# A hybrid attention block on eight cores: all GEMMs feature-major, gates per partition, norms by one ones-matmul, contiguous compression reads

## What is computed

```python
mod = jax.nn.silu(c) @ w_ada[l] + b_ada[l]                       # (B, 6D)
shift1, scale1, gate1, shift2, scale2, gate2 = [m[:, None, :] for m in jnp.split(mod, 6, axis=-1)]
h = _rmsnorm(x, norm1_g[l]) * (1.0 + scale1) + shift1
proj = h @ w_in[l]                                               # (B, T, D_IN)
nsa_q, nsa_kv, nsa_gate, fox_qkv, fox_f, merge_g = jnp.split(proj, SPLIT_POINTS, axis=-1)
...
o_nsa = _nsa(q_n, kv_n, nsa_gate, ...)      # compressed, selected and window attention, 16 heads, 4 kv groups
o_fox = _fox(q_f, k_f, qkv_f[:, :, 2], fox_f + b_forget[l])      # softmax attention with forget gates, 16 heads
g_merge = jax.nn.sigmoid(merge_g)
y = g_merge[..., :D] * (o_nsa @ w_up_nsa[l]) + g_merge[..., D:] * (o_fox @ w_up_fox[l])
x = x + gate1 * (y @ w_out[l])
h2 = _rmsnorm(x, norm2_g[l]) * (1.0 + scale2) + shift2
x = x + gate2 * (jnp.square(jax.nn.relu(h2 @ w_ff1[l])) @ w_ff2[l])
```

## Time and profile before

| what | value |
|---|---|
| median of 3 runs | 9671.58 us (9669.93 to 10086.41) |
| the profiled execution | 9690.02 us, its span 9688.5 us |
| busy in the span: TensorE, VectorE, ScalarE | 8696.5, 1708.3, 1575.5 us |
| span of the eight cores | 9649.9 to 9688.5 us |
| HBM read, written | 1604.60 MB, 138.41 MB |

### The profile page before, as it was taken

One profiled execution on the slowest core, in us unless ns is written; L12 is line 12 of the kernel. 1 busy time (PEld: TensorE's weight loads), 2 busy tenths in 40 slices (PEclk: granted clock), 3 DMA queues, 4 the chain that ended last, 5 costly groups with the idle time before them and its releaser, 6 DMA issues.

```text
span 9688.5 us, 111427 instructions; the slowest of 8 cores (9649.9 to 9688.5 us)
## 1 busy us (share of the span) xinstructions
PE 8696.5 (90%) x43283; PEld 3928.5 (41%) x43283; DVE 1708.3 (18%) x3599; ACT 1575.5 (16%) x2833; POOL 355.0 (4%) x676
## 2 busy tenths in 40 slices
PE   2287998999998887888889988999999999999999
PEld 1133333344444553333334443444444444444444
DVE  2012302210000112222222222311111111121112
ACT  2022202221002663222220011200000000000000
POOL 0000000000000000000000000000000000000000
PEclk6598998999999999999999999999999999999999
DMA  9955565785224664222224555445644764565455
GB/s 201 169 126 118 114 119 111 132 149 108 53 53 93 129 130 90 54 44 51 55 42 106 113 122 132 93 78 134 153 90 80 156 140 78 107 156 111 79 135 133
DMA packets 338516, 1049.97 MB, mean 108 GB/s; under 512 B 80928, under 2 KB 138688, under 8 KB 251728
## 3 DMA queue, kind: packets, MB, share of 16 engines
q0 software_dynamic: 96768, 700.33, 41.0%
q1 hardware_dynamic: 241232, 342.53, 11.4%
HBM read 1604.60 MB, written 138.41 MB: 180 GB/s over the span
## 4 chain that ended last, share of the span: by engine, by line
PE 79%; DMA 10%; DVE 5%; issue 3%; ACT 2%; SPq 1%; DVEq 0%; ACTq 0%; POOLq 0%
PE ps L335 78%; DMA ws_46<-w_ada 4%; DMA cx_48_90<-xc 2%; DMA rope_104<-rope 1%; DMA cx_47_89<-xc 1%; DMA ws_45<-w_inV 1%; PE ps L339 1%; SPq L371 0%; DVE onsa_141 L355 0%; DVE oaccS_140 L349 0%; DVE of_79_121 L349 0%; DVE oaccS_140 L355 0%; DMA xt_25_67<-xc 0%; DMA out<-x_131_173 0%; ACT pT_75_117 L342 0%
## 5 line engine op out<-in xcount | busy, mean ns | idle before, releaser
L335 PE MATMUL ps<-hown_61,ws_43 128*128 128x512 bf16 x2624 | 683.2, 393 | 5.5 <-DVE hown_61 L351 2.7
L335 PE MATMUL ps<-hown_61,ws_45 128*128 128x512 bf16 x2496 | 655.7, 396 | 0.0
L335 PE MATMUL ps<-hown_61,ws_44 128*128 128x512 bf16 (+1 forms) x2112 | 556.5, 399 | 0.0
L342 ACT ACTIVATE rl_157_199<-ps 128x512 f32<-128x512 f32 x128 | 76.4, 597 | 2129.2 <-PE ps L335 2129.2
L335 PEld LDWEIGHTS ps<-hown_61,ws_43 128*128 128x128 bf16 x2624 | 243.7, 100 | 256.7 <-issue 62.8
L335 PEld LDWEIGHTS ps<-hown_61,ws_45 128*128 128x128 bf16 x2496 | 233.6, 101 | 232.9 <-issue 51.1
L335 PE MATMUL ps<-ws_43,uT_189 128*128 128x512 bf16 x1408 | 321.8, 379 | 0.0
L335 PE MATMUL ps<-ws_155,uT_189 128*128 128x512 bf16 x1408 | 321.8, 379 | 0.0
L335 PE MATMUL ps<-x1T_165,ws_44 128*128 128x512 bf16 x1408 | 314.6, 382 | 4.2 <-ACT x1T_165 L342 2.6
L335 PE MATMUL ps<-x1T_165,ws_45 128*128 128x512 bf16 x1408 | 309.3, 381 | 0.0
L335 PE MATMUL ps<-wsx_201,uT_189 128*128 128x512 bf16 x1344 | 307.2, 379 | 0.0
(11 more groups left out here) (473 smaller groups left out, 10497.6 us busy)
## 6 DMA issues: line engine op xcount, KB each, us to landing
ws_44<-w_ada POOLq DMA_DIRECT2D x61, 1024.0 KB, 10.0
ws_45<-w_ada POOLq DMA_DIRECT2D x47, 1024.0 KB, 10.4
ws_44<-w_ff POOLq DMA_DIRECT2D x43, 1024.0 KB, 8.5
ws_45<-w_ff POOLq DMA_DIRECT2D x43, 1024.0 KB, 8.6
ws_43<-w_ff POOLq DMA_DIRECT2D x43, 1024.0 KB, 8.4
ws_155<-w_ff POOLq DMA_DIRECT2D x43, 1024.0 KB, 8.6
ws_43<-w_ada POOLq DMA_DIRECT2D x42, 1024.0 KB, 10.7
ws_46<-w_ada POOLq DMA_DIRECT2D x42, 1024.0 KB, 11.0
```

The lines of the kernel that those rows point to most:

```text
L335: S.emit(PE, lambda e: e.matmul(out_, lhsT, rhs, start=start, stop=stop, skip_group_check=True), reads, writes)
L342: S.emit(ACT, lambda e: e.activation(out=out_, in_=in_, func=func, **kw), reads, writes)
```

## The change

All GEMMs become feature-major. The host gives x transposed, as 32 tiles of 128 features, and takes `out` so; W_V, W_out and W_ff2 are tiled as the others.

- One `gemm` takes the place of both forms. It holds one slot; the last three column tiles of W_out and the first four of W_ff1 run as a group, half 0 of all, then half 1.
- A gate is now a column of `modT`, a scalar per partition: `stt` does product and sum in one, in W_out and W_ff2. The spread rows, `d_gate` and its loads go.
- Norms sum over partitions: squares are added up in a tile `acc` of 128 x 512 by ScalarE and VectorE (`add_square`), and one fp32 ones-matmul per 512 tokens gives the sum in all partitions (`rstd`). `modulate` is one VectorE product and one ScalarE scale and shift per 512.
- `ctx_build` loads each context tile once, 64 of 128 x 512, issued two steps ahead into three buffers. No transposes.
- `cmpx` is laid out so that a compression's operand is a run of 127.
- The rotation table: resident for q (`ropeO`); for keys three buffers loaded two ahead.
- V: `epi_v` copies on ScalarE, transposes 4 times, copies on VectorE, stores. `hold` is gone.

```diff
-    def ctx_build():
...
+        for j in range(-2, len(steps)):
+            if j + 2 < len(steps):
+                kc, t0, n = steps[j + 2]
+                x = tiles[j + 2] = cxr.next()
+                dma(SP, x.t[:, 0:n], xT_d[kc, :, t0:t0 + n], [], [x.b])
+            if j >= 0:
+                kc, t0, n = steps[j]
+                x = tiles.pop(j)
+                add_square(cacc, t0, n, x.t[:, 0:n], csq.next(), kc == 0, [x.b])
+                cp(DVE, hctx.t[:, kc, t0:t0 + n], x.t[:, 0:n], [x.b], rbs(hctx, kc, t0, n))
+            yield 1800
+        for t0, n in CC:
+            rstd(cacc, t0, n, PS[7])
+            yield 3000
+        for kc, t0, n in steps:
+            modulate(hctx, kc, t0, n, cacc, csq.next(), s1T, 0)
+            yield 1800
...
+    def gemm(srcs, ncol, places, ring, epilogue):
         ws = [slots.get(s) for s in srcs]
+        for tb, t0, n, idx in places:
+            for j, w in enumerate(ws):
+                p = ring.next()
+                for kc in range(32):
+                    mm(p.t[0:ncol, 0:n], w.t[:, ncol * kc:ncol * kc + ncol], tb.t[:, kc, t0:t0 + n], kc == 0, kc == 31,
+                       [w.b] + rbs(tb, kc, t0, n), [p.b])
+                    if kc % 2:
+                        tick(n / 1.2)
+                spawn(epilogue(p, j, idx))
+        for w in ws:
+            slots.put(w)
...
+    def add_square(acc, t0, n, x, sq, first, xb):
+        if first:
+            act(acc.t[:, t0:t0 + n], x, AF.Square, xb, [acc.b])
         else:
+            act(sq.t[:, 0:n], x, AF.Square, xb, [sq.b])
+            tt(DVE, acc.t[:, t0:t0 + n], acc.t[:, t0:t0 + n], sq.t[:, 0:n], ALU.add, [sq.b], [acc.b])
+    def rstd(acc, t0, n, bank):
+        a = acc.t[:, t0:t0 + n]
+        mm(bank.t[:, 0:n], onesf, a, True, True, [acc.b, cf.b], [bank.b])
+        act(a, bank.t[:, 0:n], AF.Ln, [epsc.b], [acc.b, bank.b], scale=1.0 / D, bias=epsc.t[:, 0:1])
+        act(a, a, AF.Exp, [], [acc.b], scale=-0.5)
...
-        cp(ACT, cmpx.t[:, g, 512 * tq:512 * tq + 512], p.t[:], [], [cmpx.bs[g], p.b])
+        cp(ACT, cmpx.t[:, g, :, k0 // 16:(k0 + n) // 16].rearrange("p a b -> p b a"),
+           p.t[:, 0:n].rearrange("p (b a) -> p b a", a=16), [], [cmpx.bs[g], p.b])
...
-            mm(v4(hp.t), w1v[:, l, :], cmpx.t[:, :, l:l + 16 * 126 + 1:16], l == 0, l == 31, [w1.b] + cmpx.bs, [hp.b])
+            mm(v4(hp.t), w1v[:, l, :], cmpx.t[:, :, l % 16, l // 16:l // 16 + 127], l == 0, l == 31, [w1.b] + cmpx.bs, [hp.b])
...
+    pre_rope = Pre(load_rope, [(k0, n) for _ in range(8) for _, _, k0, n in KC], 2)
...
+        def f(p, h, idx):
+            i, k0, n = idx
+            vb = vbr.next()
+            cp(ACT, vb.t[:, 0:n], p.t[:, 0:n], [], [vb.b, p.b])
+            yield 1500
+            vt, px = vtr.next(), Rx.next()
+            pb = PSB[id(px)]
+            for j in range(n // 128):
+                tr(pb[:, 128 * j:128 * j + 128], vb.t[:, 128 * j:128 * j + 128], ident, [vb.b, cb.b], [px.b])
...
+    def epi_out(p, ci, idx):
+        i, t0, n = idx
+        xr, x1 = pre.get(), x1r.next()
+        c = slice(0, n)
+        stt(x1.t[:, c], p.t[:, c], modT.t[:, 64 + ci:65 + ci], xr.t[:, c], ALU.mult, ALU.add,
+            [xr.b, modT.bs[(64 + ci) // 4]], [x1.b, p.b])
+        dma(SP, out[ci][:, t0:t0 + n], x1.t[:, c], [x1.b], [g_out[ci][i]])
+        cp(ACT, x1T.t[:, ci, t0:t0 + n], x1.t[:, c], [x1.b], rbs(x1T, ci, t0, n))
+        add_square(acc2[i], 0, n, x1.t[:, c], sqx.next(), ci == 0, [x1.b])
+        yield 0
+        if ci == 31:
+            spawn(norm2(i, t0, n), 1500)
```

More of the change, by code:

```diff
@@ L415, in emit_program, with region, rbs @@
     o_end = M.top - 9216
[L417 to L421, removed]
+    def region(name, off, chunks):
+        T = sum(n for _, n in chunks)
+        tb = M.at(name, [128, 32, T], BF16, off,
+                  [(2 * (kc * T + t0), 2 * (kc * T + t0 + n)) for kc in range(32) for t0, n in chunks])
+        tb.chunks = chunks
+        return tb
+    def rbs(tb, kc, t0, n):
+        k = len(tb.chunks)
+        return [tb.bs[k * kc + i] for i, (c0, m) in enumerate(tb.chunks) if c0 < t0 + n and t0 < c0 + m]
     def wslot(off):
@@ new lines, in emit_program @@
+    hctx = region("hctx", o_r2, CC)
+    cxr = Z.ring("cx", 3, [128, 512], F32)
+    csq = Z.ring("csq", 2, [128, 512], F32)
+    cacc = Z.tile("cacc", [128, sum(n for _, n in CC)], F32)
+    dma(SP, ropeO.t[:], rope_d[:, :, QOFF:NK], [], [ropeO.b])
+    def ctx_build():
+        steps = [(kc, t0, n) for kc in range(32) for t0, n in CC]
+        tiles = {}
+        for j in range(-2, len(steps)):
[15 more added lines that the diff above has]
+            yield 1800
@@ L817, in emit_program, with __init__, get @@
-    vtr = Z.ring("vt", 2, [128, 4, 4, 128], BF16)
+    rpr = Z.ring("rope", 3, [32, 2, 512], F32)
+    vbr = Z.ring("vb", 2, [128, 512], BF16)
+    vtr = Z.ring("vt", 2, [128, 4, 128], BF16)
+    class Pre:
+        def __init__(self, load, keys, ahead):
+            self.load, self.keys, self.ahead = load, keys, ahead
+            self.n, self.i, self.have = 0, 0, {}
+        def get(self):
+            i = self.i
+            self.i += 1
+            while self.n < len(self.keys) and self.n <= i + self.ahead:
+                self.have[self.n] = self.load(*self.keys[self.n])
+                self.n += 1
+            return self.have.pop(i)
@@ L861, in emit_program @@
     ZF = Bump(M, o_q, o_aend)
-    fks = [ZF.tile(f"fk{i}", [128, TCTX], BF16) for i in range(2)]
+    fks = [ZF.tile(f"fk{i}", [128, NK], BF16) for i in range(2)]
     fqs = [ZF.tile(f"fq{i}", [128, TOWN], BF16) for i in range(2)]
@@ L1469 @@
         b, half = k // 2, k % 2
-        outp[b, half * TOWN:(half + 1) * TOWN] = np.asarray(res.results[k]["out"])
+        outp[b, half * TOWN:(half + 1) * TOWN] = np.asarray(res.results[k]["out"]).reshape(D, TOWN).T
     return outp
```

542 lines of the change are left out of this document (198 added, 344 removed).

## The result

The changed kernel takes 9306.34 us (median of four, 9295.38 to 9314.51); the ratio to before is 0.9622, 95% interval 0.9599 to 0.9646. Executions in which one die ran at a lower clock than the other are left out of all times and ratios from here on; before took 9669.93 and 9671.58 us. The profiled execution took 9306.09 us, 384 less than the one of before (9690.02). Forecast were 9249 us for the median and 423 less for the profiled execution.

The account below looks back on a forecast made before the run. The prediction took TensorE's work plus what holds TensorE up as the bound. Stage terms summed to -423 us, from 9690 to 9267 for a profiled execution; the median, 18.4 below, was forecast at 9249, range 9140 to 9410.

Parts of the forecast that it names:

- q projections, 132 less: Stage from 476 to 1148 us: context loads read once and issued ahead, 672 to 540 us, with 70 us still lost.
- Were it not for SP's queue: Context loads in the q projections: a d_fq store delays the two loads behind it by up to 3 us, 68 us in all.
- context loads stay exposed: Rival: SP's order makes each of 64 loads visible in full in the q projections, stage 688 us, time 9397; 12 in 100.
- Compressions, 66 less: Compressed keys and gates, 1148 to 1509 us: contiguous operand runs save 45 us, gate rows and clock more; 361 to 295 us.
- Keys with rope, 62 less: Keys with norm and rope, 1509 to 1834 us: three rope buffers loaded two ahead end VectorE's 114 us wait; 263 us left.
- V, 6 more: V projection, 2345 to 3055 us: w_inV waits go, transposes add 21 us and ada tiles 26; 716 us (0 to 45 more).
- FoX and NSA, 55 less: FoX and the rest of NSA, 3055 to 5127 us: 33 pieces, gate rows, rows and brow waits leave (25 to 65 less).
- W_out and MLP, 112 less: W_out, MLP and end: transposes with their copy wait, 68.7 us, go; 4005 us left, with some 15 us wait in W_ff1.
- 9165 to 9390: Whole kernel: the time in us that the bounds of the terms together were said to give.
- V was not starved: Rival: in V each of 33 pieces waits for its ada tile, 330 us come back, time 9579; 4 in 100.
- that rival: DMA fills up in the context phase and the kernel is slower, 9880 at 11 us seen per load; 3 in 100.
- the waits that move: Rival: extra VectorE and ScalarE norm work holds epilogues elsewhere, giving back up to half the gain, 9460; 6 in 100.

## Why the prediction was right, and where not

*What bounds the kernel.* Right: the holes were where the stages showed them, and the operand order costs nothing. The matmul of 512 columns has a mean of 379 ns in W_ff2 before and after, here one weight tile's group on the page of the changed kernel:

```profile
L339 PE MATMUL ps<-uT_179,ws_44 128*128 128x512 bf16 x1408 | 307.5, 379 | 0.0
```

*q projections, 132 less.* This is the step that failed: its wait. "A 256 KB load from x lands in 3.4 us": that row was of a quiet stretch; beside the weight tiles it took 5.1 us, more than the lead of 3.6. "Were it not for SP's queue": with the store out of the queue the waits stayed (43.7 us), with a longer lead and more buffers they went (11.8), and the time fell by some 55 us. So loads were late by their landing, where I had only the two behind a store late, by the queue. The size came near by luck. I had 17 holes of 2.5 us, 42.5 us; TensorE sat idle for 42.6 us of the stage. I had 25 us for the lower clock; TensorE's 519 us of busy time are 49 above the 470 of work, and that is where the missing 22 us are. Some 17 of them are the clock of 0.81 on cores 4 and 5, below. The rival "context loads stay exposed" had the loads right, but blamed SP's order too, and its price of 218 us was far off: 39 to 54 us of waits over 64 loads are under 1 us for each.

By the Trainium skill, "DMA: Bandwidth & Descriptors", section "Anatomy of one DMA — SWDGE (gpsimd) path", the prediction had an estimate of about 2.6 us for such a load; that fit is for loads that GpSimd issues, and these are SP's. Here it took 5.1 us, and 8.3 with six buffers, in a stretch in which weight tiles of 1 MB land too. The measurement decides. The Trainium skill's advice on the same page, section "Bandwidth", to batch transfers to 1 MiB and more, was not tried.

*Compressions, 66 less.* The mechanism and its size are shown: some 43 us by the layout alone, where I had 45. The rest was 11 to 13 us, where I had 19 or 20 for the gate rows and the clock; 7.6 us of waits for `rows` and 2.1 for `zg` stand in the stage, which I had not counted.

*Keys with rope, 62 less.* Shown: 55 came, the load alone is worth some 50 to 55, and the clock came back with it.

*V, 6 more; FoX and NSA, 55 less.* V came out at 714 for 716, with TensorE busy 713. The pieces moved at a small profit. With `hold` put back 39 of the 47 us are lost again, the waits for `rows` among them; that the other 8 are the gate rows and the wait for `brow` is argued from the earlier trace rows, and no run takes them out alone.

*W_out and MLP, 112 less.* 116 came, 101 of them up to W_ff1's first matmul, and the wait there is 13.1 us where some 15 were forecast. But "the transposes with the wait for their copy" misnames what went: the copy stood behind a store, and the transposes put apart give some 25 us alone. The sum was right because the change ends the waits together, and I reckoned the new stage from its work, not from the wait that went.

*Sum.* 384 of 423 us came for the profiled execution. The other 18 of the 57 us between 9249 and 9306 are a step of the sum of its own: the median of before lies 18.4 us below its profiled execution, and I carried that over; after the change the two are 9306.34 and 9306.09. The time of 9306 lies inside the stated range. Its "9165 to 9390" has no working: the bounds of the terms added up give 9148 to 9536. V was not starved. The context phase did not fill the DMA queues so far that it cost the gain (share 0.70 from 480 to 680 us; that rival needs 7.7 us seen for each load). Of the waits that move, those for `rows` and `zg` and the one at W_ff1 showed, far from half the gain.

## What to carry to other kernels

Reckon a new stage from its own work and its own waits, not from the one wait that the old profile names: when it goes, another can come in its place. Ask what the engine that is waited for waited for itself. Take a transfer's landing from a stretch that is as full as the one where it will run, and give a prefetch a lead over that, with some to spare. A large refactoring is best costed stage by stage, since its parts pay in different places and each can be undone alone.

## What was not expected of the hardware

With twice the buffers the loads took longer each (5.1 to 8.3 us), and the waiting for squares still fell (38.6 to 11.8 us): here the longer lead outweighed the longer landing.

The granted clock stayed between its two levels (1.2 and 2.4 GHz) on a part of the cores. In the changed kernel, from 680 to 780 us, TensorE of core 5 is busy for the whole 100 us, at a granted clock of 0.81, and does 383 matmuls; core 7, as busy, does 464 at 1.00. In each tenth of that stretch core 5 has 0.81 and 39 or 40 matmuls, so it is no mean of high and low. The two rows, core 5 and then core 7:

```profile
680.00:780.00 100.00, 100.00 (x383) 41.44 (x381) 35.63 (x54) 55.01 (x79) 3.16 (x6) 0.81 0.35 69
```

```profile
680.00:780.00 100.00, 100.00 (x464) 45.11 (x462) 44.60 (x68) 66.47 (x97) 3.69 (x7) 1.00 0.46 91
```

Cores 4 and 5 show it, the other six don't (0.99 to 1.00). The 81 matmuls that core 5 does fewer are 17 us at 0.216 each. In the run with six steps of lead cores 0 and 1 have the same 0.81 there, and TensorE of core 0 has it from 500 us on, busy without a hole up to 780; in the run with the old layout of the compressions core 1 has 0.81 and core 0 0.79. In the MLP, from 5800 to 9200 us, all eight cores of the changed kernel run at 1.00. What holds the clock down was not found.
